# Attention over cached pages in a hybrid decoder step: the order of key and value requests, of output products, and the place of the first query layout

## Chip, cores and metric

The kernel runs on one core of a Trainium2 chip. The metric is the device time of one execution in microseconds (us), the median of several runs. A run of its own is taken with the hardware profiler, which gives the page and the trace.

## What is computed

One layer of a decoder for two groups of requests: a prompt of 256 tokens without a past, and samples, 8 sequences of 8 new tokens, each with 256 cached tokens. The layer has an mLSTM branch (4 heads of 256), a branch of forgetting attention (8 heads of 128), gates that merge them, and a mixture of 32 experts. The change touches only the attention of the samples. For it the reference says:

```python
# q (B,T,H,D); k,v (B,S,H,D): cached tokens first, then the new ones
s = jnp.einsum('bqhd,bkhd->bhqk', qb, k) * D ** -0.5
s = s + F_q[..., None] - F_k[:, :, None, :]        # sums of log forget gates
s = jnp.where(k_pos[None, :] <= pb[:, None], s, -jnp.inf)
p = jax.nn.softmax(s, axis=-1)
o = jnp.einsum('bhqk,bkhd->bqhd', p, v)

k_past = cache_k[l][page_table]                    # two pages of 128 tokens per sample
v_past = cache_v[l][page_table]
k_all = concatenate([k_past, k_b], axis=1)
v_all = concatenate([v_past, v_b], axis=1)
```

All data are float32.

## The kernel before

**Dense products.** The projections run section by section in the order of `SECTIONS`: `mo mk mq mv ga gb fk fq fv bm bf out`. A section has four chunks of 256 columns, a chunk two or three units, each a group of products into one of the banks 0 to 2. The sections `fk`, `fq`, `fv` (attention's keys, queries, values) have three units per chunk: two for the prompt (line 1746, 24 products) and one for the samples' 64 tokens (line 1732, 16 products), whose lower part is added by VectorE in line 1493 after ScalarE has copied it (line 818). `bm` and `bf` have two units per chunk (line 1742). The weights of a chunk (1 MB, line 469) are split in a high and a low part by ScalarE (line 798) and VectorE (line 1131).

**Steps between units.** Everything else is a step, hung behind a unit by `stages()`, and every engine goes through units and steps in this one order. Here (fv 2, 1) is the unit 1 of chunk 2 of section `fv`. The samples' attention has five steps for each sample b:

- FS0: VectorE copies the sample's new keys behind the cached ones, lays its queries on a diagonal (`qms`) and spreads the log forget values, ending in line 1430; semaphore `fs_ready`.
- FS1: TensorE makes the scores in bank 3 (lines 1953 to 1961) out of queries, keys and forget sums; VectorE takes the maximum, ScalarE the exponentials, VectorE normalises.
- FS2: TensorE turns the probabilities (line 1970, bank 5), VectorE lays them into `PTm` (lines 1456, 1457).
- FS3: TensorE multiplies them with the values in bank 4 (line 1988, 48 products): for each head, sources j = 0 and 1 are the two cached pages in `Vc`, j = 2 the new values in `fv`.
- FS4: the output is turned and stored in `oT`.

The prompt's attention has steps FP1 to FP3 for each head beside them; FP1 uses banks 7 and 4, FP2 (line 1934) bank 5. From (fv 3, 2) on, each unit is followed by FS3 of sample n - 2, FS2 of n - 1, FS1 of n, FS0 of n + 1, FP3, FP2, FP1 and FS4: (fv 3, 2) has FS3(0) and FS1(2), (bm 0, 0) FS3(1) and FS1(3), and so on, one sample per unit. FS0(0) and FS1(0) stand behind (fv 2, 2). Before the 16 to 48 products of a step, TensorE waits for the bank (`claim`), for what VectorE has prepared, and for the data.

**Requests.** GpSimd asks for keys and values by DMA, each sample's in two requests of 512 KB, in one queue in the order of its program. Before a pair it reads two page numbers. There are two buffers for values (b odd or even) and two for keys: one in `fm` for samples 0, 1, 3, 5, 7, one in `em` for samples 2, 4, 6, which covers memory that the dense products of `fv` read. `keys(2)` waits for the last of these (`unit_full`), the other `keys(b)` for FS1 of sample b - 2, or 0 for sample 1; `values(b)`, for b of 2 or more, for FS3 of sample b - 2 (`pe_past`). The buffers allow `keys(3)` once FS1(1) is done.

The queue before: `keys(0)`, the forget values, memsets (the last one, line 689, sets `att_zeroed`, for which FS0(0) waits), `values(0)`, then `keys(b)`, `values(b)` for b = 1 to 7, with the stores of the prompt's and samples' `v` in front of `keys(3)`.

Of the kernel before, what the change touches and what calls it, by code (L numbers as in the profile page):

```python
# [30 lines left out]
TP, BS, TS = 256, 8, 8  # L31
# [6 lines left out]
HF, DF = 8, 128  # L38
# [10 lines left out]
CPS = D // CW  # L49
# [19 lines left out]
def units_of(c):  # L69

    return 2 if SECTIONS[c // CPS] in BY_FEATURE else 3


def stages():

    order = [(c, u) for c in range(NCH) for u in range(units_of(c))]
    at = {cu: [] for cu in order}

    def after(section, chunk, unit, n=0):

        return at[order[order.index((CPS * SECTIONS.index(section) + chunk, unit)) + n]]

    for n in range(1, 6):
        after("mo", 0, 1, 1 + 3 * (n - 1)).append(("G", n, 0))
    for t in range(3):
        after("mq", 1 + t, 1).append(("KT", t, 0))

    for h in range(HM):
        after("mv", h, 2, 2 if h < HM - 1 else 1).append(("P2", 0, h))
        after("mv", h, 2).append(("P1", 0, h))  # L90
    after("ga", 0, 0).append(("F1", 0, 0))
    for h in range(HM):
        after("ga", 1, 1, h).append(("P2", 1, h))
        after("ga", 0, 1, h).append(("P1", 1, h))
    after("ga", 0, 1).append(("F3", 0, 0))
    after("ga", 1, 0).append(("F2", 0, 0))

    after("ga", 2, 1).append(("SA", 0, 0))
    after("ga", 3, 0).append(("F1", 1, 0))
    for h in range(HM):  # L100
        for b in range(BS):
            line = after("ga", 3, 1, (h * BS + b) * 9 // (HM * BS))
            line.append(("SB", h, b))
            if h == 0 and b in (4, 5, 6):
                line.extend({4: (("F2H", 1, 0),), 5: (("F2L", 1, 0), ("F2H", 1, 1)), 6: (("F2L", 1, 1),)}[b])
        if h < HM - 1:
            line.append(("SA", h + 1, 0))
    after("ga", 3, 1).append(("F3", 1, 0))
    after("fk", 0, 0).append(("F1", 2, 0))
    after("fk", 0, 1).append(("F3", 2, 0))  # L110
    after("fk", 1, 0).append(("F2", 2, 0))

    for w, section in enumerate(("fk", "fq")):
        for t in range(3):
            after(section, 3, 2, 2 * t).append(("N1", w, t))
            after(section, 3, 2, 2 * t + 3).append(("N2", w, t))

    after("fv", 2, 2).append(("FS0", 0, 0))
    for n in range(HF + 2):
        line = after("fv", 3, 0, n) if n else after("fv", 2, 2)  # L120
        line.extend((k, n - s, 0) for s, k in ((2, "FS3"), (1, "FS2"), (0, "FS1"), (-1, "FS0")) if 0 <= n - s < BS)
        line.extend((k, n - s, 0) for s, k in ((2, "FP3"), (1, "FP2"), (0, "FP1")) if 0 <= n - s < HF)
        if n >= 2:
            line.append(("FS4", n - 2, 0))
    return at
# [32 lines left out]
def hybrid_step(nc, A, O):  # L158

    AT = stages()  # L160
    fill, count = {}, {b: 0 for b in range(8)}
    for c in range(NCH):
# [6 lines left out]
    with ctx:  # L169
        handles = {}  # L170

        def sem(name):
            if name not in handles:
                
                handles[name] = ctx.enter_context(nc.semaphore(name))
            return handles[name]
# [21 lines left out]
        def take(n):  # L198
            top[0] += n
            assert top[0] <= FW, top[0]  # L200
            return fm[:, top[0] - n:top[0]]

        def cube(ap, a):
            return ap.rearrange("p (a b) -> p a b", a=a)
# [5 lines left out]
        upto, last, maskT, mask, after = take(128), take(128), take(128), take(128), take(128)  # L210
# [62 lines left out]
        fv = cube(take(3 * D), 3)  # L273
# [103 lines left out]
        def keys_of(b):  # L377

            return KTc[1 if b >= 2 and b % 2 == 0 else 0]

        def keys_landed(b):

            other = b >= 2 and b % 2 == 0
            return sem("other_keys_in" if other else "keys_in"), 16 * NPAGES * (b // 2 if other else BS + 1 + (b + 1) // 2)

        def of_head(ap, h):

            n = HF // 2
            at = DIAGQ * n * (h // n) + HQ * (h % n)
            return ap[:, at:at + HQ]  # L390

        def units(c):

            return sum(units_of(k) for k in range(c)), units_of(c)

        def n_low(c):

            return sum(units_of(k) == 3 for k in range(c))
# [5 lines left out]
        def first(section):  # L404

            return CPS * SECTIONS.index(section)
# [149 lines left out]
        def _(pool):  # L556
# [57 lines left out]
            def pe_past(st):  # L614

                b = banks_of(st)[-1]
                pool.wait_ge(sem(f"bank_full{b}"), fill[st, b] + 1)

            def out(dst, src, name):
                pool.dma_start(dst, src).then_inc(sem(name), 16)  # L620
# [10 lines left out]
            def pages(b):  # L631

                return [pool.value_load(pt[0:1, b * NPAGES + j:b * NPAGES + j + 1], min_val=0, max_val=NPHYS - 1)
                        for j in range(NPAGES)]

            def keys(b):

                if b == 2:
                    pool.wait_ge(sem("unit_full"), units(first("bm"))[0])
                elif b:  # L640
                    pe_past(("FS1", max(b - 2, 0), 0))
                for j, page in enumerate(pages(b)):
                    pool.dma_start(keys_of(b)[:, :, j * PAGE:(j + 1) * PAGE],
                                   A["cache_kT"][bass.ds(page, 1)].rearrange("a d h s -> (a d) h s"))\
                        .then_inc(keys_landed(b)[0], 16)
# [7 lines left out]
            def values(b):  # L653

                if b >= 2:
                    pe_past(("FS3", b - 2, 0))
                for j, page in enumerate(pages(b)):
                    pool.dma_start(Vc[b % 2][:, j, :], A["cache_v"][bass.ds(page, 1)].rearrange("a s f -> (a s) f"))\
                        .then_inc(sem(f"values_in{b % 2}"), 16)
# [28 lines left out]
            g(nc.gpsimd.memset(qms, 0.0))  # L688
            g(nc.gpsimd.memset(Ps[0:NS, :], 0.0), sem("att_zeroed"))
            values(0)  # L690
            for b in range(1, BS):
                if b == 3:

                    pool.wait_ge(sem("unit_free_a"), units(first("bm"))[0] - n_low(first("bm")))
                    pool.wait_ge(sem("low_added"), n_low(first("bm")))
                    out(O["v_prompt"], fv[:, 0:2, :], "v_stored")
                    out(O["v_sample"], fv[0:NS, 2, :], "v_stored")
                keys(b)
                values(b)

            pool.wait_ge(sem("o_split"), KC)
            g(nc.gpsimd.iota(iota, pattern=[[1, SLOTS]], base=0, channel_multiplier=0,
# [74 lines left out]
        def _(act):  # L777
# [108 lines left out]
            def P1(st):  # L886
                _, c, h = st
                n = c * HM + h
                if n == 0:
                    act.wait_ge(sem("gate_acts"), 2)  # L890
                if n >= 2:
                    pe_past(("P2", (n - 2) // HM, (n - 2) % HM))
                s(A_(kw[n % 2], kM(c, h), ACT.Copy, scale=ew[:, c, 8 + h:9 + h]), sem("kw_ready"))
# [9 lines left out]
            def P2(st):  # L903
                _, c, h = st
                if c == 1:
                    take_inter(st, c, h, h)
# [787 lines left out]
        def _(pe):  # L1694
# [3 lines left out]
            def claim(st, b):  # L1698

                if fill[st, b]:  # L1700
                    pe.wait_ge(sem(f"bank_free{b}"), fill[st, b])

            def full(ins, b):
                ins.then_inc(sem(f"bank_full{b}"), 1)
# [268 lines left out]

            def FS3(st):
                b = st[1]
                if b == 0:

                    pe.wait_ge(sem("unit_free_a"), units(first("fv") + CPS)[0] - n_low(first("fv") + CPS))
                    pe.wait_ge(sem("low_added"), n_low(first("fv") + CPS))
                pe.wait_ge(sem("fs_pt"), b + 1)  # L1980
                pe.wait_ge(sem(f"values_in{b % 2}"), 16 * NPAGES * (b // 2 + 1))
                claim(st, 4)
                for h in range(HF // 2):
                    for j in range(3):
                        for i in range(2):
                            g = h + HF // 2 * i
                            w = slice(DF * g, DF * (g + 1))
                            ins = mm(bank[4][HQ * i:HQ * (i + 1), 0:DF], of_head(PTm[:, j, :], g),  # L1988
                                     Vc[b % 2][:, j, w] if j < 2 else fv[:, 2, w],
                                     start=(h == 0 and j == 0), stop=(h == HF // 2 - 1 and j == 2),  # L1990
                                     skip_group_check=True)
                full(ins, 4)
# [245 lines left out]
```

## Time and profile before

| | |
|---|---|
| median of 3 runs | 853.22 us (851.37 to 853.85) |
| the profiled execution | 851.17 us, of which span of the trace 849.3 us |
| TensorE busy | 738.6 us, 87% |
| VectorE busy | 403.8 us, 48% |
| ScalarE busy | 298.3 us, 35% |
| GpSimd busy | 144.2 us, 17% |
| moved by DMA | 202.84 MB, mean 239 GB/s |

The page gives shares over the whole span, and the stages differ: dense products and mLSTM to about 383 us, attention beside the last `fv` and the `bm` products to about 505, `bf` and `out` products to about 580, the router to about 617, then the experts. So the busy shares say little about one stage; the waits, the time lines and the windows of a stretch do. In a time line a row is a run of instructions of one line: start, duration of the run, and in brackets how long the engine was idle before it and what released it. "issue" there means that the profile names no releaser. The granted clock (1.00 is 2.4 GHz) is a mean over the window of a row.

### The profile page before, as it was taken

The numbers are of one execution on the slowest core, as the hardware profiler recorded it, in microseconds if no ns is written. First come the engines' busy times: TensorE is split into PE (matmuls) and PEld (weight loads), VectorE is DVE, ScalarE is ACT, GpSimd is POOL, SyncE is SP. The second block draws the span as 40 slices with busy tenths as digits, with TensorE's granted clock in tenths as the row PEclk, the third lists the DMA queues.
The fourth block names the chain that finished last, engine by engine and source line by source line (L and its number), as shares of the span: only waits on it lengthen the run. The fifth ranks groups of instructions, "written<-read, shape, count | busy, mean of one in ns | idle before, by whom it ended". The sixth has DMA issues, their size and how long they took to land.

```text
span 849.3 us, 14573 instructions
## 1 busy us (share of the span) xinstructions
PE 738.6 (87%) x5476; PEld 592.1 (70%) x5476; DVE 403.8 (48%) x936; ACT 298.3 (35%) x550; POOL 144.2 (17%) x245
## 2 busy tenths in 40 slices
PE   2999899999999999987789999893899999777770
PEld 1799899998666798986678889882755555443430
DVE  3476233565755457584456657746642222111123
ACT  4532644465533445563222234544311111111110
POOL 5001000002433200421212100003012222212210
PEclk9999999999999999999999999997899999999995
DMA  5244343334889632736566538856399999999976
GB/s 189 100 150 144 142 141 108 102 105 183 247 247 255 219 108 104 257 101 208 178 223 227 162 109 304 352 232 237 155 421 418 419 418 418 420 419 419 419 304 193
DMA packets 38170, 202.84 MB, mean 239 GB/s; under 512 B 7490, under 2 KB 8018, under 8 KB 18898
## 3 DMA queue, kind: packets, MB, share of 16 engines
q1 hardware_dynamic: 24434, 160.29, 49.3%
q0 software_dynamic: 13664, 41.58, 15.5%
q8 instruction: 46, 0.75, 0.4%
q14 instruction: 26, 0.21, 0.1%
HBM read 184.24 MB, written 23.38 MB: 244 GB/s over the span
## 4 chain that ended last, share of the span: by engine, by line
PE 60%; DMA 18%; DVE 11%; ACT 5%; issue 4%; SPq 1%; POOLq 0%; DVEq 0%; POOL 0%; ACTq 0%
PE bank L1742 20%; PE bank L1746 10%; DMA fm<-in_w_moe 7%; DMA em<-in_w_moe 7%; PE bank L2096 6%; PE bank L1732 3%; PE bank L2116 3%; DVE rm L1131 2%; PE bank L1904 2%; ACT rm L798 2%; PE bank L1988 2%; PE bank L2077 2%; PE bank L1893 1%; DMA fm<-y_rows 1%; DMA fm<-in_w_dense 1%
## 5 line engine op out<-in xcount | busy, mean ns | idle before, releaser
L1742 PE MATMUL bank<-rm 128*128 128x320 f32 x1344 | 206.0, 312 | 2.6 <-ACT fm L826 1.6
L1742 PEld LDWEIGHTS bank<-rm 128*128 128x128 f32 x1344 | 197.4, 188 | 7.0 <-issue 3.1
L1131 DVE TENSOR_TENSOR rm<-fm,rm 128x2048 fp32r<-128x2048 f32 x48 | 110.0, 2292 | 71.8 <-ACT rm L798 71.2
L1746 PE MATMUL bank<-rm 128*128 128x256 f32 x960 | 122.3, 287 | 2.4 <-DVE fm L1522 2.4
L1746 PEld LDWEIGHTS bank<-rm 128*128 128x128 f32 x960 | 118.4, 194 | 3.3 <-issue 2.9
L798 ACT ACTIVATE rm<-fm 128x2048 fp32r<-128x2048 f32 x48 | 91.9, 1915 | 19.0 <-PE bank L1742 11.1
L2098 PE MATMUL bank<-fm,em 128*64 128x256 f32 x384 | 96.6, 397 | 0.0
L2096 PE MATMUL bank<-em 128*64 128x256 f32 x272 | 68.1, 395 | 13.4 <-DMA fm<-in_w_moe 7.9
L2096 PE MATMUL bank<-fm,em 128*64 128x256 f32 x240 | 58.9, 390 | 10.6 <-DMA fm<-in_w_moe 9.2
L2096 PEld LDWEIGHTS bank<-em 128*64 128x64 f32 x272 | 36.2, 141 | 40.4 <-issue 25.3
L1094 ACT ACTIVATE fm<-bank 64x256 f32<-64x256 f32 x32 | 12.0, 375 | 136.7 <-PE bank L2098 136.7
L732 POOL DMA_INDIRECT y_rows<-fm,im x32 | 29.2, 913 | 161.7 <-DVE fm L1648 157.4
L2096 PEld LDWEIGHTS bank<-fm,em 128*64 128x64 f32 x240 | 31.6, 139 | 33.5 <-issue 18.7
L2098 PEld LDWEIGHTS bank<-fm,em 128*64 128x64 f32 x384 | 51.4, 141 | 0.0
L663 POOL DMA_DIRECT2D fm<-in_state_C x32 | 17.6, 551 | 164.4 <-DVE fm L1284 119.1
L1653 DVE TENSOR_TENSOR fm<-bank,fm 64x256 f32<-64x256 f32 x32 | 13.6, 426 | 61.7 <-ACT fm L1094 61.6
L1732 PE MATMUL bank<-rm 128*128 128x256 f32 x320 | 42.9, 286 | 0.0
L1363 DVE SCALAR_TENSOR_TENSOR fm<-fm,bank 128x257 f32<-128x257 f32 x64 | 28.0, 479 | 30.4 <-PE bank L1904 29.5
L1660 DVE COPY fm<-bank 128x128 f32<-128x128 f32 x32 | 9.3, 291 | 68.3 <-PE bank L2107 68.2
L1732 PEld LDWEIGHTS bank<-rm 128*128 128x128 f32 x320 | 40.0, 192 | 1.6 <-DVE fm L1522 1.5
L1648 DVE COPY fm<-bank 64x512 f32<-64x512 f32 x32 | 22.2, 694 | 29.5 <-PE bank L2116 29.5
L1087 ACT ACTIVATE fm<-bank 64x512 f32<-64x512 f32 x32 | 18.9, 589 | 44.7 <-PE bank L2116 44.7
(391 smaller groups left out, 1013.4 us busy)
## 6 DMA issues: line engine op xcount, KB each, us to landing
fm<-in_w_moe SPq DMA_DIRECT2D x57, 1024.0 KB, 26.8
fm<-in_w_dense SPq DMA_DIRECT2D x48, 1024.0 KB, 4.9
em<-in_w_moe SPq DMA_DIRECT2D x39, 1024.0 KB, 26.0
fm<-in_state_C POOLq DMA_DIRECT2D x32, 257.0 KB, 5.4
out_C_sample<-fm POOLq DMA_DIRECT2D x32, 257.0 KB, 6.5
fm<-in_cache_v POOLq DMA_DIRECT2D x16, 512.0 KB, 4.5
fm<-in_cache_kT POOLq DMA_DIRECT2D x10, 512.0 KB, 5.8
em<-in_cache_kT POOLq DMA_DIRECT2D x6, 512.0 KB, 7.9
```

The lines of the kernel that those rows point to most:

```text
L732: pool.indirect_dma_start(y_rows, bass.IndirectOffsetOnAxis(ap=row_i[:, v:v + 1].bitcast(U32), axis=0), yrow[v % NY], None, bounds_check=6 ...
L798: s(A_(pair[c % 2][0], cube(raw[c % RAW1], KC), ACT.Copy), sem("hi_done"))
L1087: A_(yrow[v % NY][:, 0:D // 2], bank[4 + v % 2][0:CAP, :], ACT.Copy).then_inc(sem("e_y_left"), 1)
L1131: s(TT(pair[c % 2][1], cube(raw[c % RAW1], KC), pair[c % 2][0], ALU.subtract), sem("split_done"))
L1363: done(STT(Cout[n % NCOUT][:, k, :], Cin[n % NCIN][:, k, :], dec8[:, HM * b + h:HM * b + h + 1], bank[bk][:, 0:DE], ALU.mult, ALU.add), bk)
L1648: CP(yrow[v % NY][:, D // 2:D], bank[4 + v % 2][CAP:2 * CAP, :]).then_inc(sem("e_y_right"), 1)
L1732: ins = mm(bank[b][:, 0:CW], samp[:, k, :], w[:, k, :], start=(k == 0 and i == 0), stop=(k == KC - 1 and i == 1))
L1742: ins = mm(bank[b][:, 0:NT], w[:, k, P * u:P * (u + 1)], a[:, k, :], start=first, stop=final)
L1746: ins = mm(bank[b][0:r, 0:CW], a[:, k, TILE0[u]:TILE0[u] + r], w[:, k, :], start=first, stop=final)
L2096: last_g = mm(bank[b][0:CAP, 0:FE], x[:, k, :], g[:, k, :], start=(k == 0), stop=(k == KC - 1), skip_group_check=True)
L2098: last_u = mm(bank[b][CAP:2 * CAP, 0:FE], x[:, k, :], u[:, k, :], start=(k == 0), stop=(k == KC - 1), skip_group_check=True)
L2116: ins = mm(bank[b][CAP * j:CAP * (j + 1), :], hT[:, k, :], w[:, k, 512 * j:512 * (j + 1)], start=(k == 0), stop=(k == 1), skip_group_check ...
```

## The change

Three edits:

1. GpSimd's queue becomes `values(0)`, `keys(1)`, `values(1)`, `keys(3)`, `keys(2)`, and then `values(b)`, `keys(b + 2)` for b = 2 to 7 (keys up to 7). The stores of `v` stand in front of `values(3)`. The waits inside `keys` and `values` are as before.
2. FS3 goes through its products by source: cached page 0 for all heads, cached page 1, then the new values. For sample 0 the wait for the `fv` section (`unit_free_a`, `low_added`) moves from the head of the step in front of the products of the new values.
3. FS0(0) hangs behind (fv 2, 1) instead of (fv 2, 2).

```diff
@@ -115,7 +115,7 @@
             after(section, 3, 2, 2 * t).append(("N1", w, t))
             after(section, 3, 2, 2 * t + 3).append(("N2", w, t))
 
-    after("fv", 2, 2).append(("FS0", 0, 0))
+    after("fv", 2, 1).append(("FS0", 0, 0))
     for n in range(HF + 2):
         line = after("fv", 3, 0, n) if n else after("fv", 2, 2)
         line.extend((k, n - s, 0) for s, k in ((2, "FS3"), (1, "FS2"), (0, "FS1"), (-1, "FS0")) if 0 <= n - s < BS)
@@ -688,15 +688,20 @@
             g(nc.gpsimd.memset(qms, 0.0))
             g(nc.gpsimd.memset(Ps[0:NS, :], 0.0), sem("att_zeroed"))
             values(0)
-            for b in range(1, BS):
+            keys(1)
+            values(1)
+            keys(3)
+            keys(2)
+            for b in range(2, BS):
                 if b == 3:
 
                     pool.wait_ge(sem("unit_free_a"), units(first("bm"))[0] - n_low(first("bm")))
                     pool.wait_ge(sem("low_added"), n_low(first("bm")))
                     out(O["v_prompt"], fv[:, 0:2, :], "v_stored")
                     out(O["v_sample"], fv[0:NS, 2, :], "v_stored")
-                keys(b)
                 values(b)
+                if b + 2 < BS:
+                    keys(b + 2)
 
             pool.wait_ge(sem("o_split"), KC)
             g(nc.gpsimd.iota(iota, pattern=[[1, SLOTS]], base=0, channel_multiplier=0,
@@ -1973,15 +1978,15 @@
 
             def FS3(st):
                 b = st[1]
-                if b == 0:
-
-                    pe.wait_ge(sem("unit_free_a"), units(first("fv") + CPS)[0] - n_low(first("fv") + CPS))
-                    pe.wait_ge(sem("low_added"), n_low(first("fv") + CPS))
                 pe.wait_ge(sem("fs_pt"), b + 1)
                 pe.wait_ge(sem(f"values_in{b % 2}"), 16 * NPAGES * (b // 2 + 1))
                 claim(st, 4)
-                for h in range(HF // 2):
-                    for j in range(3):
+                for j in range(3):
+                    if b == 0 and j == 2:
+
+                        pe.wait_ge(sem("unit_free_a"), units(first("fv") + CPS)[0] - n_low(first("fv") + CPS))
+                        pe.wait_ge(sem("low_added"), n_low(first("fv") + CPS))
+                    for h in range(HF // 2):
                         for i in range(2):
                             g = h + HF // 2 * i
                             w = slice(DF * g, DF * (g + 1))
```

## Rows read from the trace of the kernel before

**Rows 1.** The page: busy share of the DMA engines in 40 slices, tenths.

```profile
DMA  5244343334889632736566538856399999999976
```

**Rows 2.** Windows: busy us of each engine, granted clock, DMA share, GB/s.

```profile
594.00:617.00 23.00, 19.01 (x116) 17.31 (x117) 14.40 (x39) 7.12 (x13) 0.61 (x1) 0.82 0.43 174
...
617.00:830.00 213.00, 185.60 (x1334) 98.64 (x1330) 49.32 (x116) 30.86 (x64) 47.86 (x62) 0.98 0.98 403
```

**Rows 3.** Waits of TensorE from 365 to 510 us: us in total, times, longest.

```profile
PE bank L1988 <- DVE fm L1493: 4.5, 1, 4.5
...
PE bank L1934 <- DVE fm L1457: 4.0, 4, 2.0
...
PE bank L1953 <- DMA fm<-in_cache_kT: 2.8, 1, 2.8
```

**Rows 4.** Time line of TensorE: start, us, line, shape, count [idle before <-releaser].

```profile
382.11 2.08 PE L1732 MATMUL bank<-rm 128*128 128x256 f32 x16
...
385.95 1.98 PE L1953 MATMUL bank<-fm 128*32 128x264 f32 x16 [1.76 <-DVE fm L1430]
...
400.00 0.24 PE L1961 MATMUL bank<-fm 128*32 128x8 f32 x4
...
404.00 2.15 PE L1732 MATMUL bank<-rm 128*128 128x256 f32 x16
...
410.68 4.48 PE L1988 MATMUL bank<-fm 128*32 128x128 f32 x48 [4.53 <-DVE fm L1493]
...
415.41 1.98 PE L1953 MATMUL bank<-em,fm 128*32 128x264 f32 x16
...
420.94 3.79 PE L1742 MATMUL bank<-rm 128*128 128x320 f32 x24
...
424.65 2.81 PE L1988 MATMUL bank<-fm 128*32 128x128 f32 x48
...
430.56 2.72 PE L1953 MATMUL bank<-fm 128*32 128x264 f32 x16 [2.77 <-DMA fm<-in_cache_kT]
...
437.70 3.79 PE L1742 MATMUL bank<-rm 128*128 128x320 f32 x24
...
450.00 3.79 PE L1742 MATMUL bank<-rm 128*128 128x320 f32 x24
...
463.83 3.79 PE L1742 MATMUL bank<-rm 128*128 128x320 f32 x24
```

**Rows 5.** Time line of VectorE, 380 to 415 us.

```profile
385.66 0.23 DVE L1430 COPY fm<-fm 128x128 f32<-128x128 f32 x1
...
406.40 0.29 DVE L1403 TENSOR_TENSOR fm<-bank,fm 128x128 f32<-128x128 f32 x1
...
410.16 0.42 DVE L1493 TENSOR_TENSOR fm<-bank,fm 64x256 f32<-64x256 f32 x1
```

**Rows 6.** Time line of GpSimd, 380 to 410 us.

```profile
381.79 0.36 POOL L689 MEMSET fm<- 64x320 f32 x1
...
407.92 1.79 POOL L643 DMA_DIRECT2D em<-in_cache_kT  x2 [12.60 <-issue]
```

**Rows 7.** Landings of the keys asked for from 407 to 410 us (sample 2).

```profile
DMA to landing us min/median/max: 4.8/5.2/5.5
```

**Rows 8.** Line 469, 395 to 440 us: the dense weights' requests and landings.

```profile
L469 SPq DMA_DIRECT2D fm<-in_w_dense x2: 328/328/328, 401.3 to 430.9; - x2
...
DMA to landing us min/median/max: 4.7/6.1/7.5
```

**Rows 9.** Landings of the keys asked for from 431 to 433.5 us (sample 4).

```profile
DMA to landing us min/median/max: 8.2/8.5/8.8
```

**Rows 10.** Windows around three waits of TensorE, columns as in rows 2.

```profile
400.00:404.00 4.00, 2.05 (x21) 1.88 (x18) 2.81 (x10) 0.74 (x4) 0.00 (x0) 1.00 0.48 124
...
410.70:414.60 3.90, 3.90 (x42) 3.90 (x44) 0.00 (x0) 0.00 (x0) 0.00 (x0) 0.56 0.74 234
...
431.60:435.10 3.50, 3.50 (x27) 2.76 (x22) 1.15 (x8) 0.00 (x0) 1.75 (x2) 0.51 0.89 330
```

## The prediction

> **What bounds the kernel now.** I read the page first, to see which resource rules which stage. The DMA row runs full from about 615 us to the end [rows 1]. In the stage before it the engines carry 174 GB/s, and in the long expert stage 403 GB/s at a share of 0.98 [rows 2]. So the experts' stage is bound by its weights, and it starts when the router is done, not at a time of its own: before it the prefetch slots are full and the DMA engines have little to do. The loads between attention and experts are each released by a TensorE, ScalarE or VectorE step. A microsecond won in attention therefore moves everything behind it by the same microsecond. I count one for one, and come back to it under what could be wrong.
>
> Then the waits of TensorE from 365 to 510 us, where the change lies. The longest is 4.5 us in front of the samples' output products (line 1988), until VectorE's line 1493; 2.8 us go to the samples' scores (line 1953) waiting for keys; 4.0 us in four pieces to line 1934, behind VectorE's line 1457 [rows 3]. The time line of TensorE gives the order. Dense products end at 384.19 (382.11 + 2.08), yet FS1 of sample 0 starts at 385.95; the dense products of `fv` end at 406.15, FS3 of sample 0 starts at 410.68, FS1 of sample 2 at 415.41, and FS1 of sample 3 at 430.56 after 2.77 us of waiting [rows 4]. TensorE is the bound of this stage wherever none of these gaps stands.
>
> **First query layout (FS0 of sample 0).** Nothing is added. Three copies on VectorE go from behind unit (fv 2, 2) to behind (fv 2, 1). Before, they stand behind line 1493, which adds the low third of that unit, and the last of them (line 1430) ends at 385.89 [rows 5]; TensorE starts 0.06 us later. After, they need only GpSimd's last memset, which ends at 382.15 [rows 6]. The three copies take 0.7 us (the last 0.23), so they end near 382.9, while the dense unit runs until 384.19. They wait on `att_zeroed`, and line 1493 is now behind that wait; it could not start before the unit's end anyway. No DMA moves with them. Gain: 385.95 - 384.20 = 1.75 us. FS1(0) releases the request of sample 1's keys, the score chain on VectorE and ScalarE, and the next dense units, so all up to the end of `fv` moves by 1.75, the dense end to 404.40.
>
> **Output products by source.** The same 384 products in another order; only sample 0 is told apart. The first 32 of its 48 use the cached values, the last 16 the new ones, and only these wait now for `fv`. The first 32 still need bank 4, freed by VectorE's line 1403 at 406.69 [rows 5], 404.94 after the shift. At full clock 48 take 2.81 us (the row at 424.65), so 32 take 1.87: 405.0 to 406.9. Line 1493 ends at 410.58 [rows 5], shifted 408.83; the last 16 then run from 408.93 to 409.87. FS3(0) so ends at 409.9, where it ended at 415.16: 4.5 us of work at the lower clock started at 410.68. By this part alone FS1(2) could start near 410.3.
>
> **What is late next: the keys of sample 2.** FS1(2) needs them, and they go into memory that the dense products of `fv` read (`keys(2)` waits for `unit_full`). Before: dense end 406.15, first request 407.92, the second 0.90 later [rows 6], and the slower of the two took 5.5 us to land [rows 7], which is 414.3, 1.1 us ahead of FS1(2). Nobody saw it. After: 404.40 + 1.77 + 0.90 + 5.5 = 412.6, and FS1(2) waits for it instead, until about 412.7 rather than 410.3. So the 5.3 us that FS3(0) gains are mostly spent on this wait. The start of FS1(2) moves from 415.41 to 412.7, 2.7 us, of which 1.75 were counted: 0.95 more.
>
> **Keys and values in the order of their buffers.** Each request is the same; GpSimd now asks for sample 3's keys before sample 2's, and from then on for keys two samples ahead. `keys(3)` waits for FS1(1), whose end at 400.24 [rows 4] becomes 398.49; its two requests (0.9 us each, 1.8 us of reading pages before) are out by 402.1. That is 2.3 us before `keys(2)` is released, so the GpSimd queue doesn't hold it up. What else is queued behind the new waits: `values(b)` stands behind `keys(b+1)`, which waits for FS1(b-1); in TensorE's order that is a unit earlier than FS3(b-2), for which `values(b)` waits anyway, so no value comes later. The stores of `v` come behind `keys(4)`, some 2 to 4 us later; the next who needs them is past 500 us. In return `keys(3)` lands near 410 for a step that comes past 424, and the 2.77 us wait at 430.56 goes. What is late next there: VectorE's bank 5 copy (line 1457) after the big split, as in three other places. I take the whole price from line lengths. The unit (bm 0, 0) with its steps lasts 437.70 - 420.94 = 16.76 us; (bm 1, 0), which has the same steps and the same split but its keys in time, 463.83 - 450.00 = 13.83 [rows 4]. Difference 2.9 us; it holds the wait, the slow clock behind it and the bank 5 wait that comes instead. The later units had no wait for keys and gain nothing.
>
> **DMA beside it.** The new cost is that `keys(3)` now shares the engines with the 1 MB of dense weights asked for at 401.3 [rows 8] (399.5 shifted) and, in its tail, with `keys(2)`. No row shows this overlap. Its bounds: nothing, or what the keys of sample 4 took: 8.8 us for the slower request, with dense weights asked for at 430.9, just ahead of them [rows 8, 9]. In between: the weights landed 4.7 us after 401.3, shifted 404.3 [rows 8]; the two requests of `keys(2)`, 0.9 us apart, landed 1.6 us apart, so the 1 MB of a sample takes some 3.2 us, and `keys(3)` would be through by 407.5 even if the weights went all ahead of it. `keys(2)` is asked for at 406.2 and 407.1; at most about 1.3 us overlap, of which one transfer gives the other half. I take 0.35 us late, near the lower bound. So 0.95 becomes 0.6.
>
> The Trainium skill speaks against the move here. "DMA: Bandwidth & Descriptors", section "Two DMAs through the same engine are not ordered", says that descriptors of one queue of an engine start in order: sample 2's keys would stand behind sample 3's, of which nobody is in need. The trace of before has sample 2's keys alone in the queue at this point and can't show it; rivals 2 and 4 below price it from rows.
>
> **TensorE's clock.** Between 410.7 and 414.6 the granted clock was 0.56 of full, practically all of it at 1.2 instead of 2.4 GHz, after 4.53 us of idleness; the same behind the wait of 2.77 us (0.51 from 431.6 to 435.1). Around the longest wait for line 1457, 2.0 us within 400 to 404, it stayed at 1.00 [rows 3, 10]. A stretch at the lower level costs 4.48 - 2.81 = 1.67 us (48 products, [rows 4]). After the change TensorE is idle from 404.4 to 412.7 but for 3.2 us in pieces of 1.9 and 1.3. That is less work than stood around 402 and about as thin as ahead of 410.7, so I take one stretch at the lower level, falling on FS1(2): 1.6 us back. Its ends are 0 and 1.67. The old fall at FS3(0) is inside the 5.3 us that count for nothing, and the one at FS1(3) is inside the 2.9.
>
> **Sum.** 1.75 + 0.6 + 2.9 - 1.6 = 3.65 us, say 3.7. The profiled execution took 851.17 us (span 849.3 and 1.9 around it), so it would be 847.5. It was the fastest of the four times known; their mean (853.22, 851.37, 853.85, 851.17) is 852.4, and since the result is a median of unprofiled runs I take 852.4 - 3.7 = 848.7.
>
> **Rivals.** (1) The clock holds: the idleness is broken into pieces of 0.6, 2.1 and 2.4 us, and two of these are no longer than others that cost nothing. Then 5.3 us, 847.1. (2) Sample 2's keys are late: they land 8.8 us after their second request at 407.07, FS1(2) starts at 416.0, 0.6 later than before; with 2.9 won and 1.6 lost 0.7 us are left, 851.7. For it speaks that the keys asked for just behind dense weights took 8.2 to 8.8 us [rows 9]; against it that the weights are 7 us ahead here. (3) The layout isn't early: if FS0(0) has to wait for `att_zeroed` past 384 us, 1.75 of the 3.7 go, 850.5. Against it stands a margin of 1.3 us. (4) Slower than before, by one mechanism: the two samples' keys don't overlap at all. `keys(3)` lands at 401.2 + 8.8 = 410.0, and only then do the keys of sample 2 take 8.8 us: 418.8, FS1(2) 3.5 us later than before; -3.5 + 2.9 - 1.6 = -2.2, so 854.6. It decides from a start of FS1(2) at 416.7, that is a landing 9.6 us after the request. No keys took so long in this trace.
>
> **How the numbers follow.** Forecast 0.40; clock holds 0.20; late keys 0.25; layout not early 0.08; slower 0.07. The likeliest gives 848.7. The range goes from rival 1 less the scatter of single runs (1.3 us around their mean), about 845.6, to just past rival 2, 852.1; outside are rival 4 and the tails. A measurement of this kernel tells about 0.3%, 2.6 us, from no change. The forecast and rival 1 lie beyond that, with a little of the late keys' weight: 0.63 faster; most of rivals 2 and 3 are within it, 0.30; slower 0.07.
>
> **What the profile after would show.** Right: FS1(0) directly behind the dense products near 384.2; line 1988 for sample 0 in two pieces, 32 and 16; a new wait of about 2.4 us at FS1(2) until its keys, in the `em` buffer; no wait for keys at FS1(3), and line 1934 waiting some 1.3 us there; the clock at half near 413 and at full near 431; landing of sample 2's keys 5 to 6.5 us. Wrong: landing over 8 us (late keys); full clock at 413 (rival 1); FS1(0) still behind line 1430; or attention shorter by the sum and the time not, which would break the one for one. That last would be a load before the experts that doesn't move with TensorE; I found none.

## The result

The changed kernel takes 848.16 us (median of 6 runs, 845.71 to 849.76), the kernel before 852.89 us beside it (6 runs, 851.37 to 853.85). The ratio is 0.9945, with a 95% interval of 0.9926 to 0.9963: about 4.7 us less, between 3.2 and 6.3. The forecast was 848.7. In a second series the same kernel gave 0.9964 (0.9945 to 0.9983), about 3.1 us less.

The profiled execution took 845.71 us, with a span of 843.8. Its time line of TensorE around the change (start, duration, line, shape, count, [idle before <-releaser]); the new lines stand five lower, so 1953, 1988, 1934, 1732, 1742 of before are now 1958, 1993, 1939, 1737, 1747:

```profile
380.92 2.08 PE L1737 MATMUL bank<-rm 128*128 128x256 f32 x16
382.93 1.98 PE L1958 MATMUL bank<-fm 128*32 128x264 f32 x16
...
395.20 3.66 PE L1958 MATMUL bank<-fm 128*32 128x264 f32 x16 [1.79 <-issue]
...
401.33 2.14 PE L1737 MATMUL bank<-rm 128*128 128x256 f32 x16
404.65 1.94 PE L1993 MATMUL bank<-fm 128*32 128x128 f32 x32 [1.17 <-DVE fm L1408]
408.26 1.07 PE L1993 MATMUL bank<-fm 128*32 128x128 f32 x16 [1.68 <-DVE fm L1498]
...
411.58 3.05 PE L1958 MATMUL bank<-em,fm 128*32 128x264 f32 x16 [1.93 <-issue]
...
418.79 3.79 PE L1747 MATMUL bank<-rm 128*128 128x320 f32 x24
...
430.07 0.52 PE L1939 MATMUL bank<-fm 128*128 128x128 f32 x3 [0.98 <-DVE fm L1462]
...
432.37 3.79 PE L1747 MATMUL bank<-rm 128*128 128x320 f32 x24
...
499.90 12.29 PE L1747 MATMUL bank<-rm 128*128 128x320 f32 x82
```

Held against [rows 4]: the scores of sample 0 follow the dense products without a gap. The output products of sample 0 run in two pieces, 32 and 16. In front of the scores of sample 2 stands a new wait. The 2.77 us for sample 3's keys are gone, and at that place line 1939 waits 0.98 us for VectorE's bank 5 copy.

The waits of TensorE from 365 to 510 us, as in [rows 3] (total, times, longest). The 4.5 us for line 1493 have become 1.7 (line 1498 now), and "issue" in front of line 1958 is sample 1's and sample 2's keys, for which this trace names no releaser:

```profile
PE bank L1958 <- issue: 3.7, 2, 1.9
PE bank L1939 <- DVE fm L1462: 2.8, 4, 1.1
PE bank L1993 <- DVE fm L1498: 1.7, 1, 1.7
PE bank L1993 <- DVE fm L1408: 1.2, 1, 1.2
```

Single executions of one kernel differ by as much as an edit here is worth (851.37 to 853.85 for the kernel before), also outside attention: the dense products of (fv 2, 2) end at 384.19 us before and at 383.00 after, though nothing ahead of them was changed. So I read a stage that begins and ends with TensorE's own work: from E, the end of the dense products of (fv 2, 2), to Z, the start of the dense products behind the last attention step. Before, Z is 505.40, so the stage lasts 505.40 - 384.19 = 121.21 us; after 499.90 - 383.00 = 116.90. That is 4.3 us. Behind Z nothing was given back in this pair. The windows from Z to the end, first of the kernel before, then of the changed one (length, busy us per engine, clock, DMA share, GB/s):

```profile
505.40:849.30 343.90, 277.39 (x1966) 184.89 (x1965) 129.99 (x286) 80.03 (x152) 57.01 (x70) 0.92 0.86 344
```

```profile
499.90:843.80 343.90, 277.37 (x1966) 184.73 (x1965) 129.98 (x286) 80.04 (x152) 57.03 (x70) 0.92 0.86 344
```

Both last 343.90 us. The span is 5.5 us shorter; 4.3 of it are the stage, 1.2 the scatter ahead of E.

### The profile page after: what moved, and what is told of

It is laid out like the page before. It is cut to its first block, busy times and chain, and to the rows that moved or that the text cites. A ratio compares the mean times of both kernels' runs of the same rounds, so it can differ in the third digit from the quotient of the medians.

```text
span 843.8 us, 14573 instructions
## 1 busy us (share of the span) xinstructions
PE 739.6 (88%) x5476; PEld 592.4 (70%) x5476; DVE 403.1 (48%) x936; ACT 298.3 (35%) x550; POOL 144.0 (17%) x245
## 4 chain that ended last, share of the span: by engine, by line
PE 62%; DMA 16%; DVE 11%; issue 5%; ACT 4%; SPq 1%; DVEq 0%; ACTq 0%; POOLq 0%
PE bank L1747 21%; PE bank L1751 11%; DMA fm<-in_w_moe 7%; DMA em<-in_w_moe 7%; PE bank L2101 6%; PE bank L1737 3%; PE bank L2121 3%; PE bank L1909 3%; DVE rm L1136 2%; ACT rm L803 2%; PE bank L2082 2%; PE bank L1898 2%; PE bank L1958 1%; PE bank L1993 1%; DMA fm<-y_rows 1%
## 5 line engine op out<-in xcount | busy, mean ns | idle before, releaser
L1665 DVE COPY fm<-bank 128x128 f32<-128x128 f32 x32 | 9.3, 291 | 68.0 <-PE bank L2112 67.9
```

## The experiments

All results in one table, each time from the profiled execution of that kernel. D is the end of the last dense products of `fv`, F the start of FS1(2), B and B1 the starts of the dense products of (bm 0, 0) and (bm 0, 1). From B1 to Z all kernels take 67.5 to 67.9 us. The ratio is to the kernel before, on the same chip, with its 95% interval. The kernel before has one profiled execution, so its row rests on that one.

| kernel | E | D - E | F - D | B - F | B1 - B | Z | Z - E | ratio |
|---|---|---|---|---|---|---|---|---|
| before | 384.19 | 21.96 | 9.26 | 5.53 | 16.76 | 505.40 | 121.21 | |
| after | 383.00 | 20.47 | 8.11 | 7.21 | 13.58 | 499.90 | 116.90 | 0.9945 (0.9926 to 0.9963) |
| y4_after, the same again | 386.43 | 20.12 | 8.26 | 6.96 | 13.58 | 502.90 | 116.47 | 0.9964 (0.9945 to 0.9983) |
| x1_layout | 383.65 | 20.14 | 9.25 | 5.53 | 16.68 | 503.16 | 119.51 | 0.9974 (0.9959 to 0.9989) |
| x2_requests | 383.89 | 21.95 | 9.68 | 5.53 | 13.58 | 502.18 | 118.29 | 0.9967 (0.9947 to 0.9986) |
| x3_source | 382.98 | 21.95 | 8.35 | 7.87 | 13.39 | 502.25 | 119.27 | 0.9984 (0.9971 to 0.9997) |
| x4_no_source | 385.43 | 20.13 | 9.21 | 5.54 | 13.59 | 501.43 | 116.00 | 0.9960 (0.9945 to 0.9975) |
| z3_no_source, the same again | 384.49 | 20.12 | 9.21 | 5.54 | 13.57 | 500.46 | 115.97 | 0.9936 (0.9912 to 0.9960) |
| y1_pages2 | 384.27 | 20.13 | 7.60 | 7.20 | 13.60 | 500.33 | 116.06 | 0.9972 (0.9953 to 0.9991) |
| y2_keys2_first | 384.96 | 20.13 | 9.26 | 7.59 | 13.60 | 503.06 | 118.10 | 0.9955 (0.9935 to 0.9975) |
| z2_keys2_pages | 385.34 | 20.12 | 7.25 | 6.96 | 13.59 | 500.80 | 115.46 | 0.9936 (0.9910 to 0.9961) |
| y3_filler | 383.83 | 20.12 | 8.56 | 5.52 | 13.59 | 499.18 | 115.35 | 0.9928 (0.9900 to 0.9956) |
| y5_pages_filler | 383.53 | 21.48 | 7.86 | 5.51 | 13.39 | 499.30 | 115.77 | 0.9949 (0.9929 to 0.9968) |
| z1_keys2_pages_filler | 383.05 | 20.13 | 7.96 | 5.53 | 13.60 | 497.80 | 114.75 | 0.9918 (0.9894 to 0.9942) |

The table shows what to trust. Where a step isn't touched and no slow clock falls on it, its length repeats to a few hundredths; the ratios, each some 0.2% wide on either side, say little more than that all are faster than before.

### One edit alone

**x1_layout**, the first query layout alone:

```diff
-    after("fv", 2, 2).append(("FS0", 0, 0))
+    after("fv", 2, 1).append(("FS0", 0, 0))
```

> Only the first query layout is moved ahead by a unit; requests and output products as before. Theory of the prediction: the 1.76 us wait of the scores of sample 0 goes, everything behind moves with it, nothing is given back, since sample 2's keys and the dense products of fv move too: 1.75 us less, a ratio of 0.998. Rival (the move feeds another wait, that of sample 1's scores for its keys, which are asked for earlier but beside the values of sample 0): 1.0 to 1.4 us less, and the wait in front of FS1(1) grows from 1.16 us by the difference.

The stage is 1.70 us shorter, D - E by 1.82; the wait in front of FS1(1) is 1.28 us. Everything else is as before to 0.2 us. The theory holds, the rival doesn't: the gain comes once and stays.

**x2_requests**, the order of the requests alone:

```diff
-            for b in range(1, BS):
+            keys(1)
+            values(1)
+            keys(3)
+            keys(2)
+            for b in range(2, BS):
...
-                keys(b)
                 values(b)
+                if b + 2 < BS:
+                    keys(b + 2)
```

> Only the order of the requests is changed; layout and output products as before. Theory: FS1(2) starts as before, its keys landing up to 0.7 us later than the 5.5 us of before but still ahead of it; the wait of 2.8 us for sample 3's keys goes and the clock stays full there; (bm 0, 0) lasts 13.6 to 13.8 us instead of 16.8: 2.9 to 3.2 us less, ratio 0.9965. Rival (keys of sample 2 held up behind those of sample 3): they land more than 6.6 us after their request, FS1(2) starts later than 9.3 us after the dense products of fv, and the gain is 1 us or none.

B1 - B falls from 16.76 to 13.58, F - D grows by 0.42; the stage is 2.92 us shorter. The theory holds. F - D is over the 9.3 us that the rival named, but not by the keys: their slower request landed after 5.4 us, near 413.9, and FS1(2) started at 415.52. The 0.42 come from the output products of sample 0, of which a longer part ran at the lower clock than in [rows 4], 4.95 us instead of 4.48:

```profile
410.32 4.95 PE L1993 MATMUL bank<-fm 128*32 128x128 f32 x48 [4.48 <-DVE fm L1498]
```

**x3_source**, the order of the output products alone:

```diff
-                if b == 0:
-
-                    pe.wait_ge(sem("unit_free_a"), units(first("fv") + CPS)[0] - n_low(first("fv") + CPS))
-                    pe.wait_ge(sem("low_added"), n_low(first("fv") + CPS))
...
-                for h in range(HF // 2):
-                    for j in range(3):
+                for j in range(3):
+                    if b == 0 and j == 2:
+
+                        pe.wait_ge(sem("unit_free_a"), units(first("fv") + CPS)[0] - n_low(first("fv") + CPS))
+                        pe.wait_ge(sem("low_added"), n_low(first("fv") + CPS))
+                    for h in range(HF // 2):
```

> Only the order of the output products, with the wait for fv in front of the last third; layout and requests as before. Theory: FS3(0) ends some 3.5 us earlier, but FS1(2) then waits for sample 2's keys and gains 1 us at most; the slow clock moves from FS3(0) to FS1(2), where it costs 1.6 us; and the wait for sample 3's keys in (bm 0, 0), whose request hangs on FS3(0) by way of values(2), gets shorter, since that request comes 3.5 us earlier: the 2.8 us wait falls to about 1 us or nothing, with its own slow clock gone or not. Sum 0 to 2 us less, ratio 0.998 to 1.000. Rival (the gain of FS3(0) reaches the end): 3.5 us less, ratio 0.996.

The stage is 1.94 us shorter, at the far end of what was expected. Its time line of TensorE, then of GpSimd:

```profile
409.51 1.07 PE L1988 MATMUL bank<-fm 128*32 128x128 f32 x16 [1.94 <-DVE fm L1493]
...
413.28 3.73 PE L1953 MATMUL bank<-em,fm 128*32 128x264 f32 x16 [2.39 <-issue]
...
432.23 0.52 PE L1934 MATMUL bank<-fm 128*128 128x128 f32 x3 [0.78 <-DVE fm L1457]
```

```profile
412.34 1.15 POOL L658 DMA_DIRECT2D fm<-in_cache_v  x2 [3.85 <-issue]
...
416.41 1.81 POOL L643 DMA_DIRECT2D fm<-in_cache_kT  x2 [1.84 <-issue]
```

D is 404.93 here. FS3(0) ends 5.65 us behind it instead of 9.0, but FS1(2) starts only 0.91 us earlier (8.35 for 9.26): it waits 2.39 us for its keys. Then its 16 products take 3.73 instead of 1.98 us, and B - F grows by 2.34. So up to B this edit alone loses 1.4 us. It wins 3.4 behind B, and by a way that has nothing to do with output products: `values(2)` waits for FS3(0), and `keys(3)` stands behind it in GpSimd's queue. With FS3(0) early, the keys of sample 3 are asked for at 416.41 and are in time. The new order of the requests (edit 1) and the new order of the output products (edit 2) remove the same wait, so only one of them can be paid for it.

**x4_no_source** and **z3_no_source**, the change without edit 2, twice:

> Layout and requests as after the change, output products by head with the wait for fv in front of all, as before it. Theory of the prediction: what the third edit wins (FS1(2) about 1 us earlier) it pays back with the slow clock on FS1(2) (1.7 us), while without it the slow clock falls on FS3(0), whose delay ends before sample 2's keys are needed only by a little; so this kernel is as fast as the changed one or up to 1 us faster: 848 us, ratio 0.993 to 0.995. Rival (the third edit carries a part of the gain): 1 to 3 us slower than the changed kernel, ratio 0.996 to 0.998.

> Once more layout and requests without the change of the output products, for its median beside the others. Its stage was 116.0 us, that of the changed kernel 116.9 and 116.5. Theory (the third edit costs on top of the other two, because its gain ends at the keys of sample 2 and the slow clock moves into the path): ratio to before 0.994 to 0.996, stage 115.9 to 116.3, and not slower than the kernel with sample 2's keys first. Rival: the difference was chance, ratio 0.996 to 0.998.

The stages are 116.00 and 115.97 us, against 116.90 and 116.47 for the whole change. On top of the other two edits, the new order of the output products costs. 0.35 of the difference to the first value are the accident in D - E, told below; the rest, 0.5 to 0.6 us, is in F - D and B - F: 8.11 + 7.21 = 15.32 and 8.26 + 6.96 = 15.22 with it, 9.21 + 5.54 = 14.75 without. The sign and the mechanism are as expected. The medians don't settle it, and x4's ratio misses the 0.993 to 0.995 that was expected (0.9960 and 0.9936 against 0.9945 and 0.9964).

```profile
409.09 4.48 PE L1993 MATMUL bank<-fm 128*32 128x128 f32 x48 [4.48 <-DVE fm L1498]
...
413.82 1.97 PE L1958 MATMUL bank<-em,fm 128*32 128x264 f32 x16
```

Here (z3) TensorE idles 4.48 us, its clock falls (0.52 of full from 409.6 to 412.9), and the lower clock is spent on FS3(0); FS1(2) follows at full speed, its keys being there.

### What holds the scores of sample 2

**y4_after**, the changed kernel again beside the next ones.

> The changed kernel as it is, beside the next ones on the same chip. Theory: the stage from the last dense product of unit (fv 2, 2) to the first behind the last attention step lasts 116.5 to 117.5 us (before: 121.2), one slow stretch of TensorE's clock falls on FS1(2), ratio to before 0.994 to 0.996. If the slow stretch falls on other steps from one execution to the next, the stage varies by up to 1.7 us with it.

Stage 116.47. FS1(1) ran at full clock here, B - F again shows one slow stretch.

**y1_pages2**, sample 2's page numbers read ahead of the wait:

```diff
             def keys(b):
 
+                early = pages(b) if b == 2 else None
                 if b == 2:
                     pool.wait_ge(sem("unit_full"), units(first("bm"))[0])
...
-                for j, page in enumerate(pages(b)):
+                for j, page in enumerate(early or pages(b)):
```

> The changed kernel, but GpSimd reads the two page numbers of sample 2 before it waits for the end of the dense products of fv, not behind. Theory (FS1(2) waits for sample 2's keys, whose request comes 1.8 us after the dense products end only because the page numbers are read behind the wait): the request follows the end by 0.1 to 0.6 us, FS1(2) starts 1.2 to 1.8 us earlier, its wait of 1.9 us shrinks to 0.1 to 0.7; with the idle time the slow clock may go too. 1.2 to 3.4 us less than the changed kernel. Rival (something else holds FS1(2), VectorE or the bank): same start of FS1(2), no gain.

The request went out 0.65 us behind D instead of 1.76 (GpSimd's rows of after, then of y1):

```profile
401.31 1.85 POOL L643 DMA_DIRECT2D fm<-in_cache_kT  x2 [9.01 <-issue]
405.23 1.75 POOL L643 DMA_DIRECT2D em<-in_cache_kT  x2 [2.06 <-issue]
```

```profile
400.20 1.79 POOL L644 DMA_DIRECT2D fm<-in_cache_kT  x2 [6.61 <-issue]
405.05 1.75 POOL L644 DMA_DIRECT2D em<-in_cache_kT  x2 [3.07 <-PE bank L1738]
```

FS1(2) came 0.5 to 0.65 us earlier. That is about half of the least that was expected, but it moved with the request, so the keys are what it waits for. The rest went into the transfer: 6.0 us to the slower landing instead of 5.4 (after) and 5.5 (y4). The wait was still 1.91 us and the slow clock came behind it. The stage is 116.06 us, 0.4 to 0.8 less than the changed kernel's where 1.2 to 3.4 were expected, and the ratio, 0.9972, shows no gain over it.

**y2_keys2_first**, the two requests exchanged:

```diff
-            keys(3)
-            keys(2)
+            keys(2)
+            keys(3)
```

> The changed kernel with sample 2's keys asked for before sample 3's. Measure: FS1(2)'s start behind the end of the dense products of fv, 8.10 and 8.26 us in two executions of the changed kernel. Theory A (the keys of sample 3, still on their way, hold back those of sample 2 by up to 1 us): landing within 5.6 us of the request, FS1(2) at 8.1 to 8.2 behind, nearly nothing gained, since most of the 8.1 us are page numbers 1.8, second request 0.9, transfer 5.5; sample 3's keys land before 420 all the same and nobody waits for them. Theory B (in-order start in the queue costs more than the bounds from the trace of before): FS1(2) at 7.5 or less. Both: stage 116 to 117 us, ratio to before 0.9945 to 0.997.

Both theories missed. FS1(2) starts 9.26 us behind D, a full microsecond later than in the changed kernel, and the stage lasts 118.10. The landings of the keys of sample 2, here and in the changed kernel:

```profile
DMA to landing us min/median/max: 4.7/5.6/6.5
```

```profile
DMA to landing us min/median/max: 4.7/5.0/5.4
```

The first request lands after 4.7 us as ever, the second after 6.5. `keys(3)` were asked for 1.4 us behind it. That they slowed it is one reading; the next run shows that the same order can also go without it. In the changed kernel `keys(3)` are asked for 3.9 us ahead of `keys(2)` (401.31 and 405.23), and the landing is no later than before, when nothing was ahead (5.5).

**z2_keys2_pages**, both together:

> The changed kernel with sample 2's keys asked for before sample 3's, and with sample 2's page numbers read ahead of the wait. With the page numbers alone the request came 1.1 us earlier but took 0.4 to 0.5 us longer. Theory A (that was sample 3's keys on the same engines): now the request follows the dense products by 0.1 to 0.7 us and lands in 5.5: FS1(2) 6.8 to 7.2 us behind them, 1.0 to 1.4 us earlier than in the changed kernel; slow clock on FS1(2) in most executions; stage 115.0 to 115.6. Theory B (the dense weights or the reading of pages hold it): FS1(2) at 7.6 as before, stage 116.

FS1(2) is 7.25 us behind D, 0.9 to 1.0 us better than the changed kernel; stage 115.46. The request went out 0.67 us behind D and landed after 5.6. With the same requests and nearly the same distances y2 needed 6.5, so theory A is right about the sum here (7.25 is just past its 7.2), but landings in this order scatter by 0.9 us between two executions, and what decides it stays open.

### What the slow clock costs

**y3_filler**: 7 products of no use in front of the products of the new values of sample 0, 8 in front of FS1(2). Each such product stands as two instructions in a time line, so 7 are x14 and 8 are x16. Those in bank 4 opened a new sum (`start=True`) while the step's own sums stood there, and the samples' output is off by a relative 0.097 with them; the likely loss is what sample 0 had summed up by then. No work is left out.

```diff
+            def filler(bk, n):
+
+                for _ in range(n):
+                    mm(bank[bk][:, 384:512], ident, ident, start=True, stop=True, skip_group_check=True)
...
+                if b == 2:
+                    filler(3, 8)
...
+                        filler(4, 7)
```

> The changed kernel with 7 products of no use in front of the output products of sample 0's new values and 8 in front of the scores of sample 2, where TensorE is idle anyway (0.215 us each at full clock; they write a part of the bank that nobody reads). Theory (the slow clock on FS1(2) comes from the thin work before it and costs 1.7 us): clock at full on FS1(2), the line from FS1(2) to the next dense product 5.5 us instead of 7.2, 1.5 us less in all. Rival (the clock falls all the same, or comes from FS1(1)'s slow stretch): the fillers run at half speed too, take 3.2 instead of 1.7 us, and the kernel gets 0 to 1.5 us slower.

B - F is 5.52 us instead of 6.96 and 7.21: full clock on FS1(2), 1.4 to 1.7 us back. F - D is 0.3 to 0.45 longer. The keys landed later (5.8 us); the trace shows no link to the products of no use, and the complete kernel z3 has 5.7 without them. Stage 115.35, 1.1 to 1.55 shorter than the changed kernel.

**y5_pages_filler**: page numbers read ahead for all samples, the 7 products only (the samples' output is off by the same 0.097).

> The changed kernel with the page numbers of every sample's keys read before the wait, and 7 products of no use in front of the output products of sample 0's new values. Theory: sample 1's keys come 1.2 to 1.8 us earlier, so the wait in front of FS1(1) goes, but VectorE's bank 5 copy then holds the next step, so that only little of it counts; sample 2's keys come 1.8 us earlier; no slow clock on FS1(2). 3 to 4 us less than the changed kernel, ratio to before 0.990 to 0.992. Rival (VectorE's chain is the bound once the keys are in time): 1 to 2 us less.

Stage 115.77, only 0.7 to 1.1 better where 3 to 4 were expected; the rival's 1 to 2 is nearer. The wait for sample 1's keys shrank to 0.71 us, and the bank 5 copy took over, with 2.16. The slow clock now fell behind that wait, on the dense products of `fv`: D - E is 21.48 for 20.12. And sample 2's keys landed only after 6.3 us, though `keys(3)` were asked for 7.7 us ahead.

```profile
401.80:405.10 3.30, 3.30 (x22) 3.17 (x23) 2.82 (x12) 0.41 (x3) 0.00 (x0) 0.64 1.01 367
```

**z1_keys2_pages_filler**, z2 with 7 and 4 such products, which open and close no sum in bank 4:

```diff
+                    mm(bank[bk][:, 384:512], ident, ident, start=start, stop=False, skip_group_check=True)
...
+                if b == 2:
+                    filler(3, 4, True)
...
+                        filler(4, 7, False)
```

> The same with 7 products of no use in front of the output products of sample 0's new values and 4 in front of sample 2's scores, writing columns that nobody reads and none that a sum stands in. Theory: full clock on FS1(2), the line from it to the next dense product 5.5 us instead of 7.0 to 7.2, FS1(2) at 7.0 to 7.3 behind the dense products of fv, stage 113.6 to 114.2 us (before: 121.2, changed kernel 116.5 to 116.9): ratio to before 0.990 to 0.992, 2.5 to 3 us faster than the changed kernel. Rival: slow clock falls elsewhere: 1 us faster.

```profile
405.74 1.83 PE L1953 MATMUL bank<-fm 128*128 128x128 f32 x14
407.73 1.07 PE L2002 MATMUL bank<-fm 128*32 128x128 f32 x16 [0.16 <-DVE fm L1499]
...
409.05 1.16 PE L1953 MATMUL bank<-fm 128*128 128x128 f32 x8
411.14 1.98 PE L1966 MATMUL bank<-em,fm 128*32 128x264 f32 x16 [0.94 <-DMA em<-in_cache_kT]
```

B - F is 5.53, full clock, as the theory says. F - D is 7.96, as the keys took 6.3 us in this execution (5.6 in z2). So the stage misses the expected 113.6 to 114.2: it is 114.75 us, 1.7 to 2.15 shorter than the changed kernel's, 6.5 shorter than before. Its median is 846.48 us against 853.80 of the kernel before beside it, ratio 0.9918. This is the fastest of the complete kernels, by the stage of one execution clearly, by the ratio with an interval (0.9894 to 0.9942) that overlaps that of the changed kernel's first series and not that of its second.

## Why the prediction was right

Its steps against the two executions of the changed kernel (saved is positive, in us):

| term | forecast | after | y4 | alone |
|---|---|---|---|---|
| first layout, D - E | 1.75 | 1.49 | 1.84 | 1.82 (x1) |
| start of FS1(2), F - D | 0.6 | 1.15 | 1.00 | 0.91 (x3) |
| slow clock on FS1(2), B - F | -1.6 | -1.68 | -1.43 | -2.34 (x3) |
| keys of sample 3, B1 - B | 2.9 | 3.18 | 3.18 | 3.18 (x2) |
| behind B1 | 0 | 0.17 | 0.15 | |
| sum | 3.65 | 4.31 | 4.74 | |

The time itself, 848.16 us against a forecast of 848.7, was hit more closely than the terms deserve. The stage says 4.3 and 4.7 us less, the sum said 3.65; the medians say 4.7 and 3.1, each to about 1.6 us. They alone couldn't have told the forecast from rival 1 (847.1). The time lines can: every step of the forecast is there.

**One for one.** The two profiles have 343.90 us each from Z to the end, so what was won was kept. That they agree to the hundredth is chance: the second execution of the changed kernel (y4) has 345.3 us there, and all fourteen lie between 343.4 and 346.8. In the five with 345.3 or more (y4, y1, y2, z2, y5) TensorE's granted clock from Z + 95 to Z + 111 us, the end of the router, is 0.85 to 0.87, in the other nine 0.91 to 0.95; what decides it is not shown. Such scatter lies in front of and behind the stage and makes the medians unsure by some 2 us: y1's stage is 5.15 us shorter than before, its median only 2.4 (0.8 to 4.0).

**First layout.** As forecast; the term was 0.26 short in one execution because the clock fell at a place that the prediction had not foreseen. In `after` the wait for sample 1's keys was 1.79 us, and FS1(1) ran at half the clock behind it:

```profile
395.50:398.60 3.10, 3.10 (x16) 1.71 (x14) 2.57 (x3) 1.13 (x3) 0.00 (x0) 0.50 0.32 132
```

Its 16 products took 3.66 us, 1.7 more. Only 0.35 of this reached D, since it used up the wait for VectorE's bank 5 copy that stood behind it (1.43 us in y4, none here).

**Output products and the keys of sample 2.** The central step, that FS3(0)'s gain is largely spent on a wait for sample 2's keys, is shown: F follows the request (y1, z2) and the landing (y2). In all nine executions with edit 2, F stands some 0.1 us behind the slower landing, whether that came after 5.4 or 6.5 us. The request came 1.76 us behind D, the slower landing 5.4 us behind it, as in the sum. The term was 0.4 to 0.55 too small, mostly because of the 0.35 allowed for sharing the DMA engines with sample 3's keys: in the two executions of the changed kernel that cost nothing (5.4 and 5.5 us to the landing against 5.5 before).

**The rule of the queue.** The rule of in-order start, quoted in the prediction against the change, isn't what these runs show to matter. With sample 3's keys ahead in the queue, those of sample 2 landed after 5.4 to 6.3 us; with them behind, asked for 1.4 us later, after 5.6, 6.3 and 6.5; without them near, after 5.5 to 5.7. That all transfers run on the same DMA engines and interleave is what the same page of the Trainium skill, "DMA: Bandwidth & Descriptors", says in its section "Issuing engines are not separate DMA queues". The trace of y2 fits this and shows no more: both samples' keys were under way there from 409.2 to 414.3 us. But the order of the requests doesn't tell who is late. Rivals 2 and 4 (late keys) were given 0.32 together; no execution had a landing over 6.5 us for sample 2.

**The clock.** One slow stretch on FS1(2), forecast by comparing the work ahead of it with that at two places of the kernel before, came in `after`, y4, y1, y2, z2 and x3, in all six executions with edit 2 and without products of no use:

```profile
412.30:415.70 3.40, 3.40 (x25) 2.43 (x23) 0.00 (x0) 0.00 (x0) 0.27 (x1) 0.51 0.81 288
```

Rival 1 (the clock holds) was too likely with 0.20. That the stretch is due to the thin work ahead and not to FS1(2) itself is shown by y3, y5 and z1: with products of no use ahead, the clock stays at 1.00 throughout FS1(2). In y5 this is so although TensorE idles for 2.92 us right before it, longer than the 2.34 of y4, behind which the clock fell. The window of y3 from FS1(2) to the next dense product:

```profile
412.50:418.00 5.50, 5.49 (x50) 4.53 (x50) 0.95 (x6) 1.17 (x6) 1.32 (x3) 1.00 0.53 192
```

**Keys of sample 3.** The price by comparison of two lines, 2.9 us, was measured as 3.18. The comparison line (bm 1, 0) itself fell by 0.16, 13.67 for 13.83, and the bank 5 wait in (bm 0, 0) is 0.98, shorter than its 1.23. In both places a request for keys no longer runs beside VectorE's copies, but that this is the reason is not shown, and x3 speaks against it: there a request (431.78 to 433.57 us) does run beside the copies of (bm 0, 0), which start at 431.35, and the wait is 0.78 us. The cause of these tenths stays open.

**What the prediction missed** is who earns what. It credited edit 2, the output products, with 0.6 less 1.6 and so, without saying it, made it a loss on top of the others; x4 and z3 show that loss, 0.5 to 0.6 us in F - D and B - F, not 1.0. And it didn't see that this edit alone would free sample 3's keys by way of `values(2)` in GpSimd's queue (x3).

## What to carry to other kernels

When a wait of an in-order engine is split or moved ahead, follow the next thing that is needed behind the freed step back to its own request. Here the output products ended 3.2 to 3.4 us earlier behind D, and the scores came only 0.9 to 1.15 earlier, held by a transfer whose request hung on the same event as before. Ask which edits remove the same wait; only their union pays, and an edit can win alone and lose beside the others. And count idle time of TensorE together with the clock: a wait of 2 us in thin surroundings cost 1.5 more, and products of no use put into it gave these back (1.4 to 1.7).

## What was unexpected of the hardware

A place ahead in the queue didn't protect a DMA request. With 1 MB of keys asked for 1.4 us behind it, it landed after 6.5 us in y2 and 6.3 in z1, but after 5.6 in z2, against 5.4 and 5.5 in the changed kernel. With these keys asked for 3.9 to 5.8 us ahead, six executions have 5.4 to 5.8 us, while y1 and y5 have 6.0 and 6.3 with 4.9 and 7.7 us between the requests. So three executions are too few to lay the late landings on the order, and what decides them stays open.

Products that open a new sum in unused columns of a bank came with a wrong result of the sums standing in its other columns: the samples' output is off by 0.097 in y3 and y5, which share only the 7 products in bank 4. The same products in the same place, neither opening nor closing a sum, left it right (z1).

Behind a wait of 1.79 us the clock fell to half (0.50) in one execution of the changed kernel, and didn't in another behind 1.66, nor behind 2.04 without edit 2 (x4); the 16 products took 3.66, 1.98 and 1.97 us. The length of the wait alone doesn't tell whether it falls.
